# Rotary half turn of the A mixers by SBUF to SBUF transfers, cosine products on GpSimd, each rotation one in-piece later

## What is computed

```python
def apply_rope(x, cos, sin):
    xf = x.astype(jnp.float32)
    x1, x2 = jnp.split(xf, 2, axis=-1)
...
    return jnp.concatenate([x1 * c - x2 * s, x2 * c + x1 * s], axis=-1).astype(x.dtype)

def diff_attention(h, w_in, w_out, lam_params, subln_g, cos, sin, layer_idx):
...
    q, k, v = jnp.split(qkv, [nq, 2 * nq], axis=-1)
    q = apply_rope(q.reshape(b, s, 2 * A_HEADS, A_HEAD_DIM), cos, sin).reshape(b, s, A_HEADS, 2, A_HEAD_DIM)
    k = apply_rope(k.reshape(b, s, 2 * A_HEADS, A_HEAD_DIM), cos, sin).reshape(b, s, A_HEADS, 2, A_HEAD_DIM)
...
        p = jax.nn.softmax(jnp.where(causal, sc, -jnp.inf), axis=-1)
        wts = p[:, :, 0] - lam * p[:, :, 1]
        return jnp.einsum('bhqk,bkhe->bqhe', wts.astype(v.dtype), v)
...
    o = rms_norm_2(o, subln_g) * (1.0 - lam_init)
    return o.reshape(b, s, A_HEADS * A_V_DIM) @ w_out
```

## Time and profile before

| | |
|---|---|
| median of 3 runs | 2416.34 us |
| lowest and highest | 2410.03, 2423.90 us |
| the profiled execution | 2411.07 us, its span 2409.0 us |
| mean granted clock of TensorE | 0.994 of full speed |
| TensorE, VectorE, ScalarE, GpSimd busy | 2348.8, 1721.8, 1191.9, 80.7 us |

### The profile page before, as it was taken

One profiled execution on the slowest core, in us unless ns is written; L12 is line 12 of the kernel. 1 busy time (PEld: TensorE's weight loads), 2 busy tenths in 40 slices (PEclk: granted clock), 3 DMA queues, 4 the chain that ended last, 5 costly groups with the idle time before them and its releaser, 6 DMA issues.

```text
span 2409.0 us, 46498 instructions
## 1 busy us (share of the span) xinstructions
PE 2348.8 (97%) x19259; PEld 2261.3 (94%) x19259; DVE 1721.8 (71%) x2265; ACT 1191.9 (49%) x1488; POOL 80.7 (3%) x163
## 2 busy tenths in 40 slices
PE   6999999999999999999999999999998999999998
PEld 6999989999999989999889999999997999988998
DVE  7888788777777867655677666676567666677665
ACT  5335865434434654433556335654354633556433
POOL 1110000000010000000000000000000000000000
PEclk9999999999999999999999999999999999999999
DMA  8987465887788533455433554335542355433552
GB/s 341 327 306 268 158 218 202 285 296 273 272 299 283 184 132 107 173 193 192 166 113 141 209 192 157 141 117 201 203 159 88 123 209 192 161 138 115 202 203 92
DMA packets 75561, 471.62 MB, mean 196 GB/s; under 512 B 8632, under 2 KB 9144, under 8 KB 26808
## 3 DMA queue, kind: packets, MB, share of 16 engines
q1 hardware_dynamic: 56288, 400.79, 46.3%
q0 software_dynamic: 18432, 67.12, 7.9%
q10 hardware_dynamic: 728, 2.14, 0.3%
HBM read 468.96 MB, written 1.05 MB: 195 GB/s over the span
## 4 chain that ended last, share of the span: by engine, by line
PE 81%; DVE 9%; ACT 3%; DMA 3%; issue 2%; POOL 0%; ACTq 0%; DVEq 0%; POOLq 0%
PE bank L2199 23%; PE bank L2201 23%; PE bank L2200 23%; DVE w_lo L1250 2%; DMA ada_wbuf<-in_ada 2%; PE bank L2210 2%; PE bank L2205 2%; PE bank L2206 1%; DVE ada_wbuf L1388 1%; DMA ARENA<-in_first 1%; ACT w_hi L622 1%; PE bank L2391 1%; PE bank L2425 1%; ACT ARENA L898 0%; DVE ARENA L1711 0%
## 5 line engine op out<-in xcount | busy, mean ns | idle before, releaser
L1250 DVE TENSOR_TENSOR w_lo<-w_raw,w_hi 128x2048 fp32r<-128x2048 f32 x371 | 849.2, 2290 | 319.4 <-ACT w_hi L622 318.2
L622 ACT ACTIVATE w_hi<-w_raw 128x2048 fp32r<-128x2048 f32 x371 | 709.1, 1914 | 509.3 <-PE bank L2201 485.7
L2199 PE MATMUL bank<-h_hi,w_hi 128*128 128x256 f32 x3376 | 942.8, 279 | 2.3 <-DVE w_lo L1250 2.3
L2201 PE MATMUL bank<-h_hi,w_lo 128*128 128x256 f32 x3376 | 934.3, 277 | 0.0
L2200 PE MATMUL bank<-h_lo,w_hi 128*128 128x256 f32 x3376 | 934.2, 277 | 0.0
L2199 PEld LDWEIGHTS bank<-h_hi,w_hi 128*128 128x128 f32 x3376 | 633.5, 188 | 9.1 <-issue 5.6
L2200 PEld LDWEIGHTS bank<-h_lo,w_hi 128*128 128x128 f32 x3376 | 633.5, 188 | 3.5 <-issue 3.4
L2201 PEld LDWEIGHTS bank<-h_hi,w_lo 128*128 128x128 f32 x3376 | 633.7, 188 | 0.0
L2199 PE MATMUL bank<-d_hi,w_hi 128*128 128x256 f32 x1920 | 536.8, 280 | 4.3 <-DVE d_lo L1616 3.3
L2201 PE MATMUL bank<-d_hi,w_lo 128*128 128x256 f32 x1920 | 532.6, 277 | 0.0
L2200 PE MATMUL bank<-d_lo,w_hi 128*128 128x256 f32 x1920 | 532.5, 277 | 0.0
(11 more groups left out here) (394 smaller groups left out, 2274.7 us busy)
## 6 DMA issues: line engine op xcount, KB each, us to landing
w_raw<-in_ws SPq DMA_DIRECT2D x371, 1024.0 KB, 4.8
ada_wbuf<-in_ada POOLq DMA_DIRECT2D x128, 512.0 KB, 5.5
ARENA<-in_first SPq DMA_DIRECT2D x8, 1024.0 KB, 19.7
work<-in_x SPq DMA_DIRECT2D x1, 1024.0 KB, 11.2
ARENA<-in_wax ACTq DMA_DIRECT2D x1, 1024.0 KB, 4.8
out_y<-ARENA SPq DMA_DIRECT2D x4, 256.0 KB, 2.1
ARENA<-in_wg ACTq DMA_DIRECT2D x1, 768.0 KB
c_rows<-in_c SPq DMA_DIRECT2D x1, 512.0 KB, 5.0
```

Of the source, the lines that this page charges most:

```text
L622: act.activation(w_hi[:, slot, :], w_raw[:, slot, :], ACT.Copy).then_inc(hi_ready, 1)
L1250: dve.tensor_tensor(w_lo[:, s, :], w_raw[:, s, :], w_hi[:, s, :].bitcast(F32), ALU.subtract).then_inc(lo_ready, 1)
L2199: pe.matmul(o, whi, xhi, start=start, stop=False, skip_group_check=True)
L2201: return pe.matmul(o, wlo, xhi, start=False, stop=stop, skip_group_check=True)
```

## The change

The eight turns of TensorE in each A mixer go. In their place ScalarE, behind each evacuation and once that has been written, issues four transfers from `raw_qk` to the new view `rot_moved` (in `sp_r`), each of 32 partitions by 2 KB, which exchange the halves. The sign goes into the sine factor (`half_sign`, one value for each partition, made by four memsets on GpSimd at the start). The product with the cosines goes from VectorE to GpSimd. In the table, rot2 to rot7 stand behind the in-piece that they preceded, and S2, S4, S6 and W0 to W3 behind them. `weigh` is as it was. Three semaphores of the opening are merged into others, which changes no order.

```diff
-    "A": """in0 in1 in2 rot0 in3 rot1 in4 S0 rot2 in5 S1 rot3 N0 in6 S2 T0 rot4 N1 in7 W0 S3 T1 rot5 N2 in8 W1 S4 T2 rot6
-            N3 in9 W2 S5 T3 rot7 N4 sq0 in10 W3 S6 T4 sum0 N5 ln0 nrm0 sq1 in11 T5 sum1 W4 S7 N6 ln1 D0.0 W5 sq2 hi0 D0.1
+    "A": """in0 in1 in2 rot0 in3 rot1 in4 S0 in5 rot2 S1 in6 rot3 N0 S2 T0 in7 rot4 N1 W0 S3 T1 in8 rot5 N2 W1 S4 T2 in9
+            rot6 N3 W2 S5 T3 in10 rot7 N4 sq0 W3 S6 T4 sum0 N5 ln0 nrm0 sq1 in11 T5 sum1 W4 S7 N6 ln1 D0.0 W5 sq2 hi0 D0.1
...
+        rot_moved = sp_r[:, :, :].rearrange("p a c -> p (a c)")[:, 0:4 * T].bitcast(F32).rearrange(
+            "p (b t n) -> p b t n", b=2, t=2)
+        half_sign = sb("half_sign", [P, 1])
...
             for st in plan.steps:
+                if st["key"][0] == "A":
+                    pool.wait_ge(rope_ready, 3 + st["key"][1])
+                    for k in range(8):
+                        pool.wait_ge(proj_ready, st["evac"] + ROT_PIECE["A"][k] + 1)
+                        if st["rots"] + k:
+                            pool.wait_ge(roped, st["rots"] + k)
+                        pool.tensor_tensor(rot_a, raw_part("A", k), cos_r.unsqueeze(1).broadcast_to([P, 2, T]),
+                                           ALU.mult).then_inc(cos_part, 1)
...
                 act.activation(dst, b, ACT.Copy, scale=0.125 if query else 1.0).then_inc(proj_ready, 1)
+                if kind == "A":
+                    act.wait_ge(proj_ready, st["evac"] + i + 1)
+                    for q in range(4):
+                        act.dma_start(rot_moved[32 * q:32 * q + 32, rot % 2, :, :],
+                                      dst[32 * (q ^ 1):32 * (q ^ 1) + 32, :, :]).then_inc(moved[rot % 2], 16)
...
-                link(dve.tensor_tensor(rot_a[:, 0:nt, :], raw_part(kind, k)[:, 0:nt, :], cosb, ALU.mult))
-                dve.wait_ge(turned, st["rots"] + k + 1)
-                m = MISC[:, 0:nt * T].rearrange("p (t n) -> p t n", t=nt)
+                if kind != "A":
+                    link(dve.tensor_tensor(rot_a[:, 0:nt, :], raw_part(kind, k)[:, 0:nt, :], cosb, ALU.mult))
+                if kind == "A":
+                    dve.wait_ge(moved[k % 2], 64 * (4 * st["key"][1] + k // 2 + 1))
+                    m = rot_moved[:, k % 2, :, :]
+                else:
+                    dve.wait_ge(turned, k + 1)
+                    m = MISC[:, 0:nt * T].rearrange("p (t n) -> p t n", t=nt)
                 link(dve.tensor_tensor(rot_b[:, 0:nt, :], m, sinb, ALU.mult))
                 chained()
+                if kind == "A":
+                    dve.wait_ge(cos_part, 8 * st["key"][1] + k + 1)
...
                     elif step == "rot":
-                        turn_pair(st, k, outs if kind == "A" else 0)
+                        if kind == "C":
+                            turn_pair(st, k)
                         rots += 1
```

More of the change, by code:

```diff
@@ L301, in build @@
         x_loaded = sem("x_loaded")
-        first_loaded = [sem(f"first_loaded{s}") for s in range(KT)]
+        first_loaded = [sem(f"first_loaded{s}") for s in range(FIRST_SLOTS)]
         first_mod = sem("first_mod")
         x_scaled = sem("x_scaled")
-        xr_T = sem("xr_T")
         c_rows_loaded = sem("c_rows_loaded")
@@ L386, in build @@
         turned = sem("turned")
+        cos_part = sem("rope_cosine_part")
+        moved = [sem(f"rope_moved{x}") for x in range(2)]
         roped = sem("roped")
@@ L509, in first @@
                     sp.wait_ge(first_used, 2 * (kt - FIRST_SLOTS) + 2)
-                sp.dma_start(first_w[:, kt % FIRST_SLOTS, :, :], a["first"][kt]).then_inc(first_loaded[kt], 16)
+                sp.dma_start(first_w[:, kt % FIRST_SLOTS, :, :], a["first"][kt]).then_inc(first_loaded[kt % FIRST_SLOTS], 16)
             def weights(n):
@@ L1633, in rotate @@
                     dve.wait_ge(rstd_ready, st["sq"] + 1)
-                    link(dve.tensor_tensor(cos_r, cos_t[:, :], rstd[:, :], ALU.mult))
-                    link(dve.tensor_tensor(sin_r, sin_t[:, :], rstd[:, :], ALU.mult))
+                    if kind == "A":
+                        dve.tensor_tensor(cos_r, cos_t[:, :], rstd[:, :], ALU.mult).then_inc(rope_ready, 1)
+                    else:
+                        link(dve.tensor_tensor(cos_r, cos_t[:, :], rstd[:, :], ALU.mult))
+                    if kind == "A":
+                        dve.wait_ge(masks_ready, 1)
+                        link(dve.scalar_tensor_tensor(out=sin_r, in0=sin_t[:, :], scalar=half_sign[:, 0:1], in1=rstd[:, :],
+                                                      op0=ALU.mult, op1=ALU.mult))
+                    else:
+                        link(dve.tensor_tensor(sin_r, sin_t[:, :], rstd[:, :], ALU.mult))
                     chained()
@@ L2375, in attention_input, with turn_pair @@
                     value_columns(st)
-            def turn_pair(st, k, units):
+            def turn_pair(st, k):
                 kind = st["key"][0]
@@ L2385, in turn_pair @@
                     pe.wait_ge(roped, st["rots"] + k)
-                if kind == "A" and st["att"] + units:
-                    pe.wait_ge(ot_ready, st["att"] + units)
-                elif kind == "C":
-                    pe.wait_ge(ot_ready, st["att"])
+                pe.wait_ge(ot_ready, st["att"])
                 m = MISC[:, 0:nt * T].rearrange("p (t n) -> p t n", t=nt)
@@ L2827, in _, with turn_rows @@
             pe.wait_ge(cols_ready, ROW_TILES)
-            def turn_rows(rows, first, done):
+            def turn_rows(rows, first):
                 for kt in range(KT):
@@ L2835, in turn_rows @@
                     if kt % 2:
-                        last.then_inc(done, 1)
+                        last.then_inc(rows_turned, 1)
             pe.wait_ge(x_loaded, 16)
-            turn_rows(x_in, 4, xin_T)
+            turn_rows(x_in, 4)
             pe.wait_ge(x_scaled, TB)
-            turn_rows(x_rows, 0, xr_T)
+            turn_rows(x_rows, 0)
             pe.wait_ge(masks_ready, 1)
```

13 lines of the change are left out of this document (8 added, 5 removed).

## The result

| | before | after |
|---|---|---|
| median, beside each other on one chip | 2419.11 us (2410.03 to 2423.90, 4 runs) | 2465.08 us (2453.95 to 2470.24, 4 runs) |
| profiled execution, its span | 2411.07, 2409.0 us | 2465.12, 2463.4 us |
| mean granted clock of TensorE | 0.994 | 0.988 |

The change makes the kernel slower: ratio 1.0192, 95% interval 1.0151 to 1.0233, so 46.0 us by the medians. The forecast was 2441, with a range up to 2456. The sign was right; the size was short by 24 us. Eighteen of these are the sum itself (46.0 against 27.8). The other six are the scale: the forecast added its 27.8 to 2413, and the kernel before measured 2419.11 beside the changed one.

What follows compares the result with a forecast made beforehand. TensorE, busy 97% of the span, was taken as the bound. Terms +0.7 − 3.2 + 4.1 + 0.6 + 2.8 + 3 × 3.0, carried as 13.9 a mixer, gave +27.8 and a forecast of 2441 us, range 2426 to 2456.

Steps and rivals of the forecast that it cites:

- (b): Start of each A mixer: ScalarE's transfer issues, 0.43 each, delay rstd and the low half; in3 starts 0.7 us later.
- (a): TensorE, each A mixer: eight turns go; seven of 0.46 save 3.2 us, the first is counted with the start.
- (e): Rotations behind VectorE's low halves: TensorE waits 4.1 us at S2, 0.6 at T0, 2.8 at W0, 3.0 at W1 to W3.
- everything stands as before: Behind W3 no rotation is left, so all stands as before relative to TensorE: no further delay.
- (c): Cosine product on GpSimd: at most 1.1 us, hidden, taking 0.61 off VectorE for each rotation.
- rival 2: VectorE and GpSimd hold each other up: 3 us a mixer, 6 in all, 2447 us; chance 0.17.
- (d): Transfers of 256 KB a rotation take 2.1 to 4.8 us, hidden if landed within 6.0 of their issue.
- Rival 3: Transfers late, at 11.2 us each: 7.5 us a mixer, 15 in all, 2456 us; chance 0.07.
- rival 1: VectorE finishes the low half in time, so no new waits: 2406 us profiled scale, 2411 median scale; chance 0.09.

Runs made afterwards that it cites:

- e7: Changed kernel with ScalarE issuing the transfers of pieces 0 and 1 later, behind rstd and the column factors: 2446.53 us in one run.
- e5: Changed kernel with unused matmuls filling TensorE's waits ahead of S2 and W0 to W3: 2459.54 us, ratio 1.0173.
- e6: Changed kernel with the cosine product back on VectorE, GpSimd idle in the A mixers: 2463.37 us in one run.
- e3: Changed kernel with VectorE's low halves behind weights and rotation, and weights ahead of the rotation: 2430.77 us, ratio 1.0065.
- e1: Kernel before with only the new order table; turns and products as they were, no transfers: 2456.64 us against 2414.82, ratio 1.0170.
- e11: Changed kernel with low halves behind weights and rotation, GpSimd issuing transfers and doing the cosine product, no rotation wait in weigh: 2408.75 us, ratio 0.9973.
- e9: Changed kernel with GpSimd issuing all transfers ahead of its product, ScalarE none: 2448.19 us in one run.

## Why the prediction was wrong in size

The wait behind the low halves was there as forecast. What failed is the rest of the sum: it ran every product of TensorE at full speed without a word on the clock (0 in the sum, 3.9 us in the first mixer), it took 0.43 for an issue that takes 0.61 (1.75), and it had GpSimd's product "hidden", where it blocked VectorE (2.7).

The delay against before, counted from the first evacuation of the mixer, at the places of the sum (first mixer; forecast worked out from its terms):

| start of | forecast | measured | step of the sum |
|---|---|---|---|
| in3 | +0.7 | +2.45 | (b) |
| S0 | +0.2 | +2.84 | (a), one turn less; half clock in in3 |
| S2 | +3.4 | +6.35 | (e), 4.1 of waiting: was 5.15 |
| W0 | +6.4 | +10.26 | (e), 0.6 and 2.8: were 0.4 and 1.8; N0 1.1 late |
| W1 | +8.9 | +13.35 | (e), 3.0 |
| W2 | +11.5 | +16.43 | (e), 3.0 |
| W3 | +14.0 | +20.29 | (e), 3.0; S at half clock |
| T5 | +14.0 | +21.96 | "everything stands as before"; half clock |

The 8.0 that are missing divide by these lines: issues 1.75 (in3); half clock 1.5 (in3 again, seen at S0), 0.7 (W2 to W3) and 1.7 (T5); GpSimd's product 1.0 (W0) and 0.5 to 0.6 at each of W1, W2 and W3; less 0.4 for the rest, in which the turns count for −0.7. These prices are read from the steps of one profile. The runs that take one cause away give other sums, since the rest moves with it: 6.7 and 6.3 for the issues at the start (e7), 2.0 and 2.7 for part of the clock (e5), and no gain for the product (e6), where the clock fell more often.

- **(e), right as a mechanism, and shown:** waits at S2 and ahead of every W, ended by the rotation; with e3 those at W1 and W3 are gone, the one at S2 is down to 0.7, and W0 and W2 wait 2.7 and 1.1, now for a transfer. W waits 1.8, 2.96, 2.96 and 2.92 (2.8 and three times 3.0 forecast). That the 3.0 was met so closely is partly luck: the loop is 0.57 longer than forecast, and about as much of it is spent in the wait of T (0.52), which the forecast did not have. The rows of the sum itself give 11.24 and 8.34, a wait of 2.9. e1 with its +19.0 and +21.3 is this term with the clock.
- **(b) failed, +1.75:** "I take 0.43" an issue. It was 0.61 (0.51 to 0.72 over all 64). The row I read the earlier trace rows was of other loads, and its longest, 0.59, was still below. The high part of in3, behind eight issues, came 5.51 later instead of 3.75, and in3 started late by that difference. Then in3 ran at half clock for 3.4 us (+1.5 against the same part of e11). e7 and e9 show the cause: with the issues elsewhere both waits are gone.
- **(c) failed by rival 2:** 1.27 for GpSimd's product against the 1.1 assumed is harmless; that it *excludes* VectorE is not. L1774 went from 0.23 to 1.31 (e6 brings it back to 0.23 with the transfers still there), and the loop from W to W is 11.87 at full clock against 11.3, which is the 0.55 that the rival had priced. Both signs that the prediction named for this came: waits that end with N, and instructions of N stretched beside the product. At W0, with no W ahead of S2, the whole 1.08 counts: S2's maxima start 2.88 behind S2, also in e5, where S2 runs at full clock. It goes both ways, as the start of the mixer shows:

```profile
1206.47 2.29 DVE L1268 TENSOR_TENSOR w_lo<-w_raw,w_hi 128x2048 fp32r<-128x2048 f32 x1
1206.70 3.22 POOL L608 TENSOR_TENSOR ARENA<-ARENA,hid 128x512 f32<-128x512 f32 x1 [1.42 <-DVE ARENA L1692]
1208.68 1.79 DVE L1676 TENSOR_TENSOR ARENA<-sp_r,hid 128x512 f32<-128x512 f32 x1
```

The product, 1.27 elsewhere, began in a low half and took 3.22, to 1209.92; the sine product of rot1, 0.68 elsewhere, took 1.79 and ended 0.55 behind it. That is what the Trainium skill says ("SBUF — State Buffer", section "SBUF: two separate sides"), and the traces agree. Its chance of 0.17 was too low. No row spoke against the rule, and the product starts with N each time.
- **(a) was undersized in the other direction:** 0.46 a turn where e11 shows 0.86. Eight turns give 3.1 more than I carried.
- **The clock was missing altogether.** Stretch less idle is the time that TensorE needed: 80.87 and 83.8 in after, 72.25 and 72.5 in e11, which has the same work. The 8.6 and 11.3 between them are about half of 17.1 and 23.9, the time at half clock. But this is not what the clock cost: part of it lies under the next wait. What does not is 1.5 in in3, the last line of the table (+1.67, half of 3.4 us) and most of the step W2 to W3 (12.59 instead of 11.87), together 3.9. e5, which kept the clock up from W0 to in11 but not at the start, won 2.0 and 2.7. So a wait can cost its length and some of the slow time behind it, not all.
- **(d) held** in after: no wait of TensorE or of a rotation ends with a transfer, though the median landing of 4.0 is near my upper value. In e3, where no low half stands ahead of the rotation, W0 and W2 wait for one. Rival 3 did not come about, nor did rival 1.

Read on TensorE alone, the first mixer divides into idle +20.1, turns −6.8 and half clock +8.6, where the forecast had +17.7, −3.7 and 0. That these make 21.9 is no proof, since the last two are both differences to e11. The checks are that 6.8 is eight times 0.85, beside the 0.86 of a single turn, and that 8.6 is half of 17.1.

## What to carry to other kernels

Moving a step on one engine moves it past everything that stands between on the others: look in the program order of the engine that feeds the bottleneck for what now stands ahead of it, and put the long work that nobody waits for (here a low half wanted two pieces later) behind the short work that somebody does. Something slow, such as a transfer, can hide behind that long work, so look for it when the work has moved. A wait on TensorE can cost more than its length where the granted clock falls behind it. Work moved from VectorE to an idle GpSimd is not free: each blocked the other here. Where transfers replace compute, count their issues at the price that this engine shows for this shape, and have an idle engine issue them.

## What of the hardware was not expected

- An issue of a transfer inside SBUF, 32 partitions of 2 KB each, holds ScalarE for 0.61 (0.51 to 0.72), GpSimd for 0.50 (e9); loads of small tensors had held ScalarE for 0.34 to 0.59.
- Such a transfer lands 1.9 to 5.7 us after its issue, median 4.0, beside the weight loads; the whole 256 KB output had taken 2.1.
- Two VectorE instructions of one value a row took 1.31 us beside GpSimd's product, and 0.23 without it (e6).
- TensorE's granted clock fell to its lower level for 3.4 or 6.8 us (10.2 around S2 in e7 and e9) during or behind waits, most of them of 1.9 to 6.2 us, and stayed there when TensorE was fully busy again; behind W0 and W1 of the first mixer of after, with waits of 1.8 and 2.96, it did not fall.
- One turn cost TensorE 0.4 beyond its own step of 0.45 (8.79 before against 7.93 in e11).
